# A hybrid decoder layer on one core: the split matrix products run high by high, high by low, low by high over all rows, instead of all three row by row

## The chip, the cores and the metric

One core of a Trainium2 chip runs the whole kernel. The metric is the device time of one execution in microseconds. In the text PE is TensorE, DVE is VectorE, ACT is ScalarE, POOL is GpSimd and SP is SyncE, which here only issues DMAs.

## The reference, cut to what matters

One layer of a decoder is computed for 1024 prompt tokens and 32 sample tokens, 1056 in all, with a model width of 1024. Everything is float32. The large products are these:

```
z = h @ w_in + b_in                                   # 1024 x 8192
q, f, i, og, glu_a, glu_b, gate_a, gate_b = split(z)
o_a = gated recurrence (HGRN2) of q, f, i, og         # small products per head
o_b = depthwise convolution of glu_a * sigmoid(glu_b), LayerNorm, silu
merged = [sigmoid(gate_a) * o_a, sigmoid(gate_b) * o_b] @ w_out     # 2048 x 1024
x = x + g1 * merged
gg, uu = split(h2 @ w_ffn_in)                         # 1024 x 5632
x = x + g2 * ((silu(gg) * uu) @ w_ffn_out)            # 2816 x 1024
y = rmsnorm(x, norm_final_w)
```

## The kernel before, in words

The wide products keep near float32 precision by splitting. A matrix A is rounded to `A_hi`, a shorter float (type fp32r), and `A_lo = A - A_hi`. A product is then the sum of `w_hi * x_hi`, `w_hi * x_lo` and `w_lo * x_hi`, three matmuls in place of one.

**Blocks.** The weights come in blocks of up to 8 row tiles of 128 rows by 128 columns (512 KB). For each block SP loads `w_raw`, ACT rounds it to `w_hi` (line 1776), and DVE, in a few places POOL, subtracts to get `w_lo` (lines 1281 and 2071). Each of these buffers exists twice, so while PE computes block b, block b+1 is prepared. ACT may write `w_hi` of block b only when block b-2 is done on PE, and SP may load into `w_raw` only when `w_lo` of block b-2 has been formed. The semaphore `w_hi_ready` counts the `w_hi` written, `w_split` the `w_lo`.

**The helper.** Every wide product after the first two tiles goes through `products` (line 865). It waits for `w_split`, and then runs over the row tiles `kt` of the block; for each row tile it issues high by high, high by low and low by high, each for all of its outputs. All matmuls have 128 rows, 128 columns of weights and 352 moving columns (`GW`, a third of the tokens), and each loads its own weights. Between row tiles it can call `at_slot`, which puts a small piece of other PE work (a "fill" of the recurrence, of the LayerNorm or of a norm) between the matmuls. `before_row` puts a wait ahead of a row tile.

**The stages.** (1) z: 64 tiles of the `w_in` product, each with three outputs in three PSUM banks (token groups g = 0, 1, 2), 72 matmuls per tile, for 8 heads of 7 tiles each and 8 tiles of `gate_b`; 62 of these go through `products`. Fills of the recurrence of the head before stand after row tiles 1, 3, 5 and 7. Before a tile is begun, PE waits for `z_free` of the tile two back, which the last reader of that PSUM tile gives. (2) Out: the `w_out` product, 3 token groups by 8 output tiles, each of two blocks (`kk`), with one output bank, 48 matmuls per tile. Its moving operand is `m_hi`/`m_lo`; at the first tile of a group PE waits row tile by row tile for `m_split`, which counts the `m_lo` that DVE formed (line 1539) from the `m_hi` of ACT (line 1942). (3) FFN: per token group 22 hidden tiles of two blocks each, then 8 output tiles of three blocks, one output bank per block. The first output tile of a group waits row tile by row tile for `a_ready`, the `act_lo` of the hidden tiles.

The program of each engine is a fixed order written out by hand, with loops (`Fori`) over heads and FFN tiles; semaphores alone tie the engines together.

## Time and profile before

| what | value |
|---|---|
| median of 3 runs | 2021.12 us (2020.4 to 2024.62) |
| profiled execution's own time | 2020.5 us |
| its span | 2018.8 us |
| PE busy | 1954.4 us, 97% of the span |
| PE weight loads busy | 1893.1 us, 94% |
| DVE busy | 1304.5 us, 65% |
| ACT busy | 671.3 us, 33% |
| POOL busy | 235.1 us, 12% |
| wide matmuls through line 876 | 10368 |

A row of the profile names the line, the engine, the operation and the tiles (output<-inputs). `PE` rows are matmuls and `PEld` rows the weight loads that run beside them. Matmuls overlap: a row's duration is longer than the distance to the next row's start, and the rate of PE is read from the starts. A bracket at a row's end gives the time that the engine had been idle and what released it.

### The profile page before, as it was taken

The page shows a single profiled execution, that of the slowest core. Times are in us where ns is not written, and L with a number is a line of the kernel's source. Part 1 is how long each engine was busy: PE and PEld are TensorE (multiplying, and loading weights), DVE is VectorE, ACT ScalarE, POOL GpSimd, SP SyncE. Part 2 cuts the span into 40 slices and gives each one's busy share as a digit, 9 for nine tenths or more (in the row PEclk, how much of TensorE's full clock was granted, in tenths as well). Part 3 has the DMA queues.
Part 4 walks back from the last instruction along what each step waited for, and adds up shares of the span by engine and source line. Part 5 has one row for each costly group of instructions (what it writes and reads, how often), then busy time and mean ns, then how long its engine had stood idle before and what let it go on. Part 6 is the DMA issues. An engine that isn't in the chain of part 4 may idle for free.

```text
span 2018.8 us, 39824 instructions
## 1 busy us (share of the span) xinstructions
PE 1954.4 (97%) x16182; PEld 1893.1 (94%) x16182; DVE 1304.5 (65%) x1800; ACT 671.3 (33%) x1090; POOL 235.1 (12%) x256
## 2 busy tenths in 40 slices
PE   7889999999999999999989989999999999999998
PEld 6888999999999999998989989999999999999998
DVE  6577969796978788887565655544446544455443
ACT  5211314132222313133664423333343333333333
POOL 2200010101010101011122484600000000000000
PEclk8999999999999999999999989999999999999999
DMA  8522232322222223223267634444444544444443
GB/s 244 193 71 68 65 89 65 85 69 69 75 78 75 79 64 88 65 65 97 89 211 215 193 100 136 137 141 136 135 138 136 155 132 137 136 142 150 142 127 113
DMA packets 417242, 237.40 MB, mean 118 GB/s; under 512 B 16375, under 2 KB 411287, under 8 KB 417072
## 3 DMA queue, kind: packets, MB, share of 16 engines
q1 hardware_dynamic: 416672, 234.48, 39.7%
q8 instruction: 115, 1.88, 0.4%
q10 hardware_dynamic: 416, 0.72, 0.1%
q14 instruction: 39, 0.32, 0.0%
HBM read 211.91 MB, written 24.11 MB: 117 GB/s over the span
## 4 chain that ended last, share of the span: by engine, by line
PE 82%; DVE 8%; ACT 3%; DMA 3%; POOL 2%; issue 1%; SPq 0%; DVEq 0%; ACTq 0%; POOLq 0%
PE Z L876 71%; DVE yb L1429 2%; PE R L900 2%; PE R L956 1%; DVE w_lo L1281 1%; PE Z L841 1%; PE R L906 1%; ACT w_hi L1776 1%; DVE ta L1446 1%; PE R L982 1%; PE R L989 1%; DMA mbuf<-merged_scratch 1%; DVE k L1310 1%; DMA w_raw<-in_w_in_dram 1%; PE R L991 1%
## 5 line engine op out<-in xcount | busy, mean ns | idle before, releaser
L876 PE MATMUL Z<-h_hi,w_hi 128*128 128x352 f32 x2544 | 684.3, 332 | 17.4 <-DVE w_lo L1281 9.7
L876 PE MATMUL Z<-h_hi,w_lo 128*128 128x352 f32 x2544 | 660.9, 323 | 0.0
L876 PE MATMUL Z<-h_lo,w_hi 128*128 128x352 f32 x2544 | 660.0, 323 | 0.0
L1776 ACT ACTIVATE w_hi<-w_raw 128x1024 fp32r<-128x1024 f32 (+1 forms) x316 | 329.3, 1042 | 962.7 <-PE Z L876 912.7
L1281 DVE TENSOR_TENSOR w_lo<-w_raw,w_hi 128x1024 fp32r<-128x1024 f32 (+1 forms) x305 | 378.6, 1241 | 393.3 <-ACT w_hi L1776 385.6
L876 PEld LDWEIGHTS Z<-h_hi,w_hi 128*128 128x128 f32 x2544 | 442.5, 189 | 36.9 <-issue 19.3
L876 PEld LDWEIGHTS Z<-h_hi,w_lo 128*128 128x128 f32 x2544 | 454.3, 189 | 0.0
L876 PEld LDWEIGHTS Z<-h_lo,w_hi 128*128 128x128 f32 x2544 | 452.4, 189 | 0.0
L1429 DVE SCALAR_TENSOR_TENSOR yb<-up,vec,yb 128x1024 f32 (+1 forms) x240 | 308.3, 1284 | 28.7 <-DVE yb L1429 3.7
L876 PE MATMUL Z<-act_hi,w_hi 128*128 128x352 f32 x528 | 170.9, 324 | 0.0
L876 PE MATMUL Z<-act_hi,w_lo 128*128 128x352 f32 x528 | 169.6, 321 | 0.0
L876 PE MATMUL Z<-act_lo,w_hi 128*128 128x352 f32 x528 | 169.3, 321 | 0.0
L876 PEld LDWEIGHTS Z<-act_hi,w_lo 128*128 128x128 f32 x528 | 99.4, 188 | 0.0
L876 PEld LDWEIGHTS Z<-act_lo,w_hi 128*128 128x128 f32 x528 | 99.2, 188 | 0.0
L876 PEld LDWEIGHTS Z<-act_hi,w_hi 128*128 128x128 f32 x528 | 99.0, 188 | 0.2 <-DVE w_lo L1281 0.2
L2154 POOL TENSOR_TENSOR gate<-ta,tb 128x1056 f32<-128x1056 f32 x8 | 20.9, 2615 | 668.1 <-ACT ta L1845 668.1
L1689 DVE TENSOR_TENSOR tb<-ta,Z 128x352 f32<-128x352 f32 x66 | 34.4, 521 | 74.3 <-PE Z L876 74.1
L876 PE MATMUL Z<-m_hi_b,w_hi 128*128 128x352 f32 x192 | 64.3, 335 | 4.5 <-POOL w_lo L2071 4.2
L876 PE MATMUL Z<-m_hi_a,w_hi 128*128 128x352 f32 x192 | 63.2, 329 | 3.5 <-DVE m_lo_a L1539 2.2
L876 PE MATMUL Z<-m_hi_b,w_lo 128*128 128x352 f32 x192 | 63.4, 330 | 0.0
L876 PE MATMUL Z<-m_lo_b,w_hi 128*128 128x352 f32 x192 | 63.2, 329 | 0.0
L876 PE MATMUL Z<-m_hi_a,w_lo 128*128 128x352 f32 x192 | 62.6, 326 | 0.0
(298 smaller groups left out, 2106.5 us busy)
## 6 DMA issues: line engine op xcount, KB each, us to landing
w_raw<-in_w_ffn_in_dram SPq DMA_DIRECT2D x132, 512.0 KB, 3.8
w_raw<-in_w_in_dram SPq DMA_DIRECT2D x64, 512.0 KB, 5.0
w_raw<-in_w_out_dram SPq DMA_DIRECT2D x48, 512.0 KB, 3.9
w_raw<-in_w_ffn_out_dram SPq DMA_DIRECT2D x48, 512.0 KB, 3.7
aw<-in_w_ada_dram SPq DMA_DIRECT2D x32, 512.0 KB, 4.0
w_raw<-in_w_ffn_out_dram SPq DMA_DIRECT2D x24, 384.0 KB, 3.3
ada_w<-in_w_ada_dram SPq DMA_DIRECT2D x16, 512.0 KB, 5.4
mbuf<-merged_scratch SPq DMA_DIRECT2D x32, 176.0 KB, 4.0
```

The lines of the kernel that those rows point to most:

```text
L841: last = mm(Z[b][:, g, 0:GW], w[:, kt, :], x[:, kt, g * GW:(g + 1) * GW], start=kt == 0 and m == 0, stop=kt == NJ - 1 and m == 2)
L876: last = mm(out, w[:, kt, :], x(kt, g), start=first and kt == 0 and m == 0, stop=last_block and kt == n - 1 and m == 2)
L900: return transpose(out, in_, ident[0:m, 0:m])
L906: last = mm(bank[group:group + 32, ADA_COL:ADA_COL + P], ct[:, kt, :], aw[:, kt, :], start=kt < 4, stop=kt >= 4)
L956: last = mm(bank[p:p + BAND, c * w:(c + 1) * w], k[:, t:t + BAND], halves(qd[:, t:t + BAND], 1 << lv, 1), start=True, stop=True)
L982: last = mm(bank[:, c * P:(c + 1) * P], ktok[:, cc, :], vtok[:, cc, :], start=True, stop=True)
L989: last = mm(out, att[:, cc, :], vtok[:, cc, :], start=True, stop=cc == 0)
L1281: st.tell(V.tensor_tensor(w_lo[b.par][:, 0:n, :], w_raw[b.par][:, 0:n, :], w_hi[b.par][:, 0:n, :].bitcast(F32), ALU.subtract), w_split, b. ...
L1429: ins = V.scalar_tensor_tensor(yp, xp, w, yp, ALU.mult, ALU.add)
L1689: st.tell(V.tensor_tensor(a, sg, Z[t.par][:, 1, 0:GW], ALU.mult), *zfree(t))
L1776: A(w_hi[b.par][:, 0:n, :], w_raw[b.par][:, 0:n, :], ACT.Copy).then_inc(w_hi_ready, 1)
L2154: st.tell(Q.tensor_tensor(gate[:, :], ta[:, :], tb[:, :], ALU.mult), gate_ready, h.v)
```

## The change

The row loop of `products` moves inside. The three kinds of product are now the outer loop, then the outputs, then the row tiles: all `w_hi * x_hi` of the block, then all `w_hi * x_lo`, then all `w_lo * x_hi`. The wait for `w_split` moves ahead of the third kind; ahead of the first stands a wait for `w_hi_ready`. Fills stay at the same count of matmuls within a block. In the z stage, where a block has three outputs, each output now gets its eight row tiles one after the other. The row waits are split likewise: `hi_row` waits for `m_hi_ready` or `a_hi_ready`, `lo_row` for `m_split` or `a_ready`. The first two z tiles, which have their own loop, are as before.

```diff
-            def products(b, outs, n, hi, lo, first, last_block, at_slot=None, slots=(), before_row=None):
+            def products(b, outs, n, hi, lo, first, last_block, at_slot=None, slots=(), hi_row=None, lo_row=None):
                 whi, wlo = w_hi[b.par], w_lo[b.par]
-                pe.wait_ge(w_split, b.v + 1)
-                for kt in range(n):
-                    if before_row is not None:
-                        before_row(kt)
-                    for m, (w, x) in enumerate(((whi, hi), (whi, lo), (wlo, hi))):
-                        for g, out in enumerate(outs):
+                count = 0
+                for m, (w, x, before_row) in enumerate(((whi, hi, hi_row), (whi, lo, lo_row), (wlo, hi, None))):
+                    if m == 0:
+                        pe.wait_ge(w_hi_ready, b.v + 1)
+                    if m == 2:
+                        pe.wait_ge(w_split, b.v + 1)
+                    for g, out in enumerate(outs):
+                        for kt in range(n):
+                            if before_row is not None:
+                                before_row(kt)
                             last = mm(out, w[:, kt, :], x(kt, g), start=first and kt == 0 and m == 0,
                                       stop=last_block and kt == n - 1 and m == 2)
-                    if kt == n - 1:
-                        last.then_inc(block_done, 1)
-                    for s in range(slots.count(kt)):
-                        at_slot()
+                            count += 1
+                            if count == 3 * len(outs) * n:
+                                last.then_inc(block_done, 1)
+                            if count % (3 * len(outs)) == 0:
+                                for s in range(slots.count(count // (3 * len(outs)) - 1)):
+                                    at_slot()
...
                              kk == 0, kk == 1, (lambda: x2_fill(g - 1, j)) if beside else None, (5,) if beside else (),
+                             (lambda kt: pe.wait_ge(m_hi_ready, M2 * g + NJ * kk + kt + 1)) if j == 0 else None,
                              (lambda kt: pe.wait_ge(m_split, M2 * g + NJ * kk + kt + 1)) if j == 0 else None)
...
-                def hidden(kk):
-
-                    return lambda kt: pe.wait_ge(a_ready, NF * g + 8 * kk + kt + 1)
+                def hidden(ready, kk):
+
+                    return lambda kt: pe.wait_ge(ready, NF * g + 8 * kk + kt + 1)
...
-                                 before_row=hidden(kk) if n == 0 else None)
+                                 hi_row=hidden(a_hi_ready, kk) if n == 0 else None,
+                                 lo_row=hidden(a_ready, kk) if n == 0 else None)
```

PE's program at a tile of the z stage, before (`h_hi` and `h_lo` are the moving operand, the numbers behind `w_hi` and `w_lo` tell the two buffers apart):

```order
244 L876 MATMUL Z<-h_hi,w_hi_68 128x352 [waits w_split,z_free1]
245 L876 MATMUL Z<-h_hi,w_hi_68 128x352 x2
246 L876 MATMUL Z<-h_lo,w_hi_68 128x352 x3
247 L876 MATMUL Z<-h_hi,w_lo_70 128x352 x3
248 L876 MATMUL Z<-h_hi,w_hi_68 128x352 x3
249 L876 MATMUL Z<-h_lo,w_hi_68 128x352 x3
250 L876 MATMUL Z<-h_hi,w_lo_70 128x352 x3
```

The same program in the changed kernel, at such a tile:

```order
177 L880 MATMUL Z<-h_hi,w_hi_68 128x352 [waits w_hi_ready,z_free1]
178 L880 MATMUL Z<-h_hi,w_hi_68 128x352 x23
179 L880 MATMUL Z<-h_lo,w_hi_68 128x352 x24
180 L880 MATMUL Z<-h_hi,w_lo_70 128x352 [waits w_split]
181 L880 MATMUL Z<-h_hi,w_lo_70 128x352 x23
```

The wait for `w_split` has moved from ahead of the first of 72 matmuls to ahead of the 49th; the wait for `z_free` stays at the first, and each x3 over three banks has become x8 in each bank.

PE's program at the begin of the out stage, before (`m_hi_a` and `m_hi_b` are the moving operands of a tile's two blocks):

```order
1406 L876 MATMUL Z<-m_hi_a,w_hi_67 128x352 [waits m_split,w_split,z_free0]
1407 L876 MATMUL Z<-m_lo_a,w_hi_67 128x352
1408 L876 MATMUL Z<-m_hi_a,w_lo_69 128x352
1409 L876 MATMUL Z<-m_hi_a,w_hi_67 128x352 [waits m_split]
1410 L876 MATMUL Z<-m_lo_a,w_hi_67 128x352
1430 L876 MATMUL Z<-m_hi_b,w_hi_68 128x352 [waits m_split,w_split]
1431 L876 MATMUL Z<-m_lo_b,w_hi_68 128x352
1432 L876 MATMUL Z<-m_hi_b,w_lo_70 128x352
```

The same place in the changed kernel:

```order
804 L880 MATMUL Z<-m_hi_a,w_hi_67 128x352 [waits m_hi_ready,w_hi_ready,z_free0]
805 L880 MATMUL Z<-m_hi_a,w_hi_67 128x352 [waits m_hi_ready] x7
806 L880 MATMUL Z<-m_lo_a,w_hi_67 128x352 [waits m_split] x8
807 L880 MATMUL Z<-m_hi_a,w_lo_69 128x352 [waits w_split]
808 L880 MATMUL Z<-m_hi_a,w_lo_69 128x352 x7
809 L880 MATMUL Z<-m_hi_b,w_hi_68 128x352 [waits m_hi_ready,w_hi_ready]
810 L880 MATMUL Z<-m_hi_b,w_hi_68 128x352 [waits m_hi_ready] x7
811 L880 MATMUL Z<-m_lo_b,w_hi_68 128x352 [waits m_split] x8
812 L880 MATMUL Z<-m_hi_b,w_lo_70 128x352 [waits w_split]
```

All eight row tiles of `m_hi` are now needed before the first of `m_lo`, and the low by high products come last.

## Rows read from the trace of the kernel before

**Rows 1.** The page, chain that ended last, by line.
```profile
PE Z L876 71%; DVE yb L1429 2%; PE R L900 2%; PE R L956 1%; DVE w_lo L1281 1%; PE Z L841 1%; PE R L906 1%; ACT w_hi L1776 1%; DVE ta L1446 1%; PE R L982 1%; PE R L989 1%; DMA mbuf<-merged_scratch 1%; DVE k L1310 1%; DMA w_raw<-in_w_in_dram 1%; PE R L991 1%
```
**Rows 2.** Waits of PE: who waited for whom, us in total, times, longest.
```profile
PE Z L876 <- DVE w_lo L1281: 11.1, 6, 5.9
...
PE Z L876 <- POOL w_lo L2071: 4.2, 1, 4.2
...
PE Z L876 <- DVE m_lo_a L1539: 2.2, 1, 2.2
```
**Rows 3.** Timeline, first wide tile: start us, us, engine, line, operation, tiles [idle<-releaser].
```profile
78.94 1.06 ACT L1776 ACTIVATE w_hi<-w_raw 128x1024 fp32r<-128x1024 f32 x1 [7.13 <-DMA w_raw<-in_w_in_dram]
79.90 1.12 ACT L1829 ACTIVATE tb<-Z,vec 128x1056 f32<-128x1056 f32 x1
80.03 1.23 DVE L1281 TENSOR_TENSOR w_lo<-w_raw,w_hi 128x1024 fp32r<-128x1024 f32 x1 [8.40 <-ACT w_hi L1776]
...
81.37 0.50 PEld L876 LDWEIGHTS Z<-h_hi,w_hi 128*128 128x128 f32 x2 [6.17 <-ACT tb L1829]
```
**Rows 4.** Timeline, third and fifth wide tile.
```profile
110.32 1.22 DVE L1281 TENSOR_TENSOR w_lo<-w_raw,w_hi 128x1024 fp32r<-128x1024 f32 x1 [9.68 <-ACT w_hi L1776]
...
128.26 0.95 PE L876 MATMUL Z<-h_hi,w_hi 128*128 128x352 f32 x2 [4.68 <-DVE q L1467]
```
**Rows 5.** Timeline, begin of the out stage, each engine.
```profile
1023.93 3.19 ACT L1942 ACTIVATE m_hi_a<-x 128x352 fp32r<-128x352 f32 x8
1024.51 5.12 DVE L1539 TENSOR_TENSOR m_lo_a<-x,m_hi_a 128x352 fp32r<-128x352 f32 x8 [0.18 <-ACT m_hi_a L1942]
1029.56 7.92 DVE L1539 TENSOR_TENSOR m_lo_b<-x,m_hi_b 128x352 fp32r<-128x352 f32 x8
1030.87 1.04 ACT L1776 ACTIVATE w_hi<-w_raw 128x1024 fp32r<-128x1024 f32 x1
1034.67 0.66 PE L876 MATMUL Z<-m_hi_b,w_hi 128*128 128x352 f32 x1 [4.24 <-POOL w_lo L2071]
1035.83 0.50 ACT L1942 ACTIVATE m_hi_b<-x 128x352 fp32r<-128x352 f32 x1 [2.50 <-POOL x L2188]
```
**Rows 6.** Windows: us, busy us (x) of PE, PEld, DVE, ACT, POOL, granted clock, DMA.
```profile
1034.60:1040.50 5.90, 5.83 (x24) 5.83 (x25) 4.01 (x6) 1.44 (x2) 1.19 (x2) 0.62 0.67 203
```
**Rows 7.** Timeline, two later tiles of the out stage.
```profile
1067.73 0.43 PE L876 MATMUL Z<-m_hi_b,w_hi 128*128 128x352 f32 x1 [0.26 <-DVE w_lo L1281]
...
1086.20 1.06 ACT L1776 ACTIVATE w_hi<-w_raw 128x1024 fp32r<-128x1024 f32 x1 [2.72 <-DMA w_raw<-in_w_out_dram]
...
1088.66 0.40 PE L876 MATMUL Z<-m_hi_a,w_hi 128*128 128x352 f32 x1 [1.17 <-DVE w_lo L1281]
```
**Rows 8.** Timeline, FFN stage, the two tiles that waited.
```profile
1520.77 0.40 PE L876 MATMUL Z<-h_hi,w_hi 128*128 128x352 f32 x1 [0.39 <-DVE w_lo L1281]
...
1779.85 0.40 PE L876 MATMUL Z<-h_hi,w_hi 128*128 128x352 f32 x1 [0.63 <-DVE w_lo L1281]
```
**Rows 9.** Timeline of PE, z stage between two fills, first and last of five.
```profile
515.24 0.64 PE L876 MATMUL Z<-h_lo,w_hi 128*128 128x352 f32 x3
...
517.18 0.65 PE L876 MATMUL Z<-h_hi,w_lo 128*128 128x352 f32 x3
```
**Rows 10.** Timeline of PE, out stage, first and last of 19.
```profile
1113.97 0.32 PE L876 MATMUL Z<-m_hi_a,w_hi 128*128 128x352 f32 x1
...
1116.87 0.32 PE L876 MATMUL Z<-m_hi_a,w_hi 128*128 128x352 f32 x1
```
**Rows 11.** Timeline of PE, FFN group 0, first and last of 27.
```profile
1299.80 0.32 PE L876 MATMUL Z<-h_hi,w_hi 128*128 128x352 f32 x1
...
1303.93 0.32 PE L876 MATMUL Z<-h_hi,w_lo 128*128 128x352 f32 x1
```
**Rows 12.** Timeline of PE, FFN group 1, first and last of 27.
```profile
1649.70 0.32 PE L876 MATMUL Z<-h_hi,w_hi 128*128 128x352 f32 x1
...
1653.86 0.32 PE L876 MATMUL Z<-h_hi,w_lo 128*128 128x352 f32 x1
```

More of the change, by code:

```diff
@@ L862, in _, with z_tile @@
             first_tiles()
-            def products(b, outs, n, hi, lo, first, last_block, at_slot=None, slots=(), before_row=None):
+            def products(b, outs, n, hi, lo, first, last_block, at_slot=None, slots=(), hi_row=None, lo_row=None):
                 whi, wlo = w_hi[b.par], w_lo[b.par]
-                pe.wait_ge(w_split, b.v + 1)
-                for kt in range(n):
-                    if before_row is not None:
-                        before_row(kt)
-                    for m, (w, x) in enumerate(((whi, hi), (whi, lo), (wlo, hi))):
-                        for g, out in enumerate(outs):
+                count = 0
[8 more added lines that the diff above has]
+                                before_row(kt)
                             last = mm(out, w[:, kt, :], x(kt, g), start=first and kt == 0 and m == 0,
                                       stop=last_block and kt == n - 1 and m == 2)
-                    if kt == n - 1:
-                        last.then_inc(block_done, 1)
-                    for s in range(slots.count(kt)):
-                        at_slot()
-            def z_tile(b, at_slot=None, slots=(), before_row=None):
+                            count += 1
[4 more added lines that the diff above has]
+                                    at_slot()
+            def z_tile(b, at_slot, slots):
                 t = b
@@ L887, in z_tile @@
                          lambda kt, g: h_hi[:, kt, g * GW:(g + 1) * GW], lambda kt, g: h_lo[:, kt, g * GW:(g + 1) * GW],
-                         True, True, at_slot, slots, before_row)
+                         True, True, at_slot, slots)
             def small(fill):
```

## The prediction

> **What bounds the kernel now.** I read the page first, then PE's waits, then the timeline around each wait, then PE's starts in undisturbed stretches. The chain that ended last is 71% wide matmuls of line 876 [rows 1], and PE is busy for 97% of the span: the kernel is a stream of 10368 equal matmuls with few holes. Two things can move it: the holes that the new waits close, and the distance between starts within the stream. One nanosecond more or less per matmul is 10.4 us, more than all the holes of this kind together.
>
> The holes that the change aims at are small. PE waited 11.1 us in 6 places for DVE's `w_lo`, 4.2 us in one for POOL's, and 2.2 us in one for `m_lo_a` [rows 2]: 17.5 us. What counts is what would be late next in each.
>
> **The holes, one by one.**
>
> *First wide tile.* `w_hi` was there at 78.94 + 1.06 = 80.00, `w_lo` at 80.03 + 1.23 = 81.26, and the weight load began at 81.37, 0.11 later. But the tile writes into the bank that ACT was reading into `tb` until 79.90 + 1.12 = 81.02 [rows 3], and the wait for `z_free` stays. The new start is about 81.12. Of 5.9 us only 0.25 is gained, the rest was the DMA.
>
> *Third to fifth tile.* The third tile waited for its `w_lo` too, but the fifth waited 4.68 us for DVE's `q`; DVE works without a pause from 110.32 to it, and what started DVE was a `w_hi` that came with its DMA [rows 4]. Starting the third tile earlier only lengthens that wait: 0.
>
> *The other z tiles.* The list has no further wait for `w_lo` there. Fills keep their place by count, and DVE's order is as before: 0.
>
> *Begin of the out stage.* Before, the first block followed `m_lo_a` row tile by row tile and ended three matmuls after the last, near 1030.3, and the second waited for POOL's `w_lo` until 1034.67 [rows 5]. Now the first block's high pass starts at about 1024.45, behind the first `m_hi`, and is paced by ACT to 1023.93 + 3.19 = 1027.1; the low pass is paced by DVE to 1024.51 + 5.12 = 1029.6; then come eight more matmuls, 1.3 us: end at 1031.1, 0.8 later than before. The second block needs `w_hi` (1030.87 + 1.04 = 1031.9), runs seven row tiles, and waits for the eighth `m_hi_b`, made at 1035.83 + 0.50 = 1036.33, where before that row was asked for last. Its low pass waits for the last `m_lo_b` at 1029.56 + 7.92 = 1037.5 at the least, and the third pass takes 1.3: end at 1039.0, against 1040.5 before [rows 6], a gain of 1.4. Before, this block ran at a granted clock of 0.62 [rows 6], its slow matmuls 0.293 us apart where the fast ones are 0.160. If after the new hole of 2.9 us it runs at the half clock again, 16 matmuls at 0.293 are 4.7 us, and the end is 1041.2: a loss of 0.8. I take half of the first: 0.7.
>
> *Later in the out stage.* A row lasts two steps, 0.32 us, so a hole in the starts is the idle time plus one step of 0.16. At 1067.73 it is 0.26 + 0.16 = 0.4, and `w_lo` caused it [rows 7]: gained, since `w_lo` is now due 16 matmuls, 2.5 us, after the start. At 1088.66 `w_hi` itself was late with its DMA, done at 1086.20 + 1.06 = 1087.26 [rows 7]; PE can start at 1087.37: 1.3 gained, `w_lo` and the next load come no later.
>
> *FFN.* The hole ahead of 1520.77 is 0.39 + 0.16 = 0.55, that ahead of 1779.85 0.63 + 0.16 = 0.8 [rows 8]. `w_hi` was long there; both go. The row waits for `act_hi` and `act_lo` caused none before, and the last hidden tile is asked for 5 matmuls into the third block, 7.7 + 0.8 us on: none now.
>
> Sum: 0.25 + 0.7 + 0.4 + 1.3 + 0.55 + 0.8 = 4.0 us. Ends: 2.5 (out stage at its worst) and 4.7. If each closed hole opened again as another wait, 0.
>
> More register work and waits on PE stand in the loops. The sequencer runs ahead of the stream, and waits that are met ride on a weight load; no row shows a cost: 0.
>
> **The step.** Starts between which nothing intervenes lie at different distances. z: 12 matmuls from 515.24 to 517.18 are 161.7 ns each [rows 9]; of the fourteen such stretches from 500 to 560 us nine read so, five near 160.0, mean 161.1. Out: 18 steps in 2.90 us, 161.1 [rows 10]. FFN group 0: 26 steps in 4.13 us, 158.8 [rows 11]. Group 1: 26 in 4.16, 160.0 [rows 12]. The granted clock is full in all. DVE, ACT and POOL being busy or not makes no difference that I could find. After an interruption the stream locks at one of three rates and keeps it until the next. The changed order has another pattern (the same kind eight times, and in z one bank at a time instead of three in turn), so the trace of before does not show its rate. Present weights: z 4464 at 161.1, FFN groups 0 and 2 3168 at 158.8, group 1 1584 and out 1152 at about 160.0, together 1660.0 us, mean 160.1. Bounds: all at 158.8 is 13.6 us less, all at 161.1 is 10.3 more, all at z's 161.7 is 16.4 more. I take 160.0, the middle rate and nearest to the mean: z loses 4.9, groups 0 and 2 gain 3.8, in all 1.1 less.
>
> The Trainium skill, page TensorE: Matmul & The Clock Gate, section "Wait — 56ns, not 53.3ns?", has a start-to-start distance of columns over 2.4 GHz plus a fixed 2.5 ns, which no order of the matmuls would alter; for 352 columns that is an estimate of 149.2 ns, and these rows are 10 to 12 ns above and differ among themselves. By that rule the step term is nil and the sum is the holes alone.
>
> **Sum.** The profiled execution took 2020.5 us, 0.6 under the median. 2020.5 - 4.0 - 1.1 = 2015.4 us, 0.28% under the median. A difference of 0.2%, 4.0 us, is about what a measurement of this kernel can tell from none: faster is under 2017.1, slower over 2025.2.
>
> **Rivals.**
> - *The step does not depend on the order*, each stage keeps its rate: 2020.5 - 4.0 = 2016.5. For it: the same operations with the same loads. Against it: rates that differ between stages now. (The page's rule above gives this one.)
> - *All streams lock at the fast rate* of FFN group 0: 2020.5 - 4.0 - 13.6 = 2002.9. For it: one bank per pass is now true everywhere, and the longest undisturbed stretches with one bank are at 158.8. Against it: group 1 and the out stage, with one bank, are not.
> - *All lock slow*, at 161.1 or above, slower than before. The place is the FFN stage, where 3168 matmuls now run at 158.8 and lose 7.3; with group 1 and out it is 10.3, 2020.5 - 4.0 + 10.3 = 2026.8, and up to 2033 at 161.7. It decides from a common step of 160.9 (8.7 us more). For it: the out stage shows 161.1 with one bank; every weight load is now a new one, where before two matmuls in a row shared `w_hi`. Against it: loads are issued for each matmul anyway.
> - *The change doesn't do what it says*: the holes move (to `z_free`, to `m_hi_b`, to the next DMA) and nothing is gained: about 2020. The first tiles are such a case already; the four later holes have no second wait that I can find.
>
> **Chances.** Forecast (2011 to 2019) 0.40; step unchanged 0.20; fast lock, and half-way to it, 0.15; slow lock 0.14; holes only move 0.11. From these: faster 0.32 + 0.11 + 0.15 = 0.58; slower the slow lock's, 0.14; same the rest, 0.28. The range leaves out the ends of both locks: 2004 to 2026. The forecast's own range is 2011 to 2019.
>
> **What would show it.** PE's waits for `w_lo` after the first tile gone, the weight load of the first wide tile begun for ACT's `tb`, the wait for `q` at 128 still there and longer; a hole ahead of the last `m_hi_b` row near 1033; no hole where 1067, 1088, 1520 and 1779 were. Starts in the z stage 160 ns apart, in FFN group 0 up from 158.8. I am wrong if the FFN groups lie at 161 or at 158 throughout, or if PE's total of waits does not fall by some 4 us.

## The result: slower by 0.24%

| | median | runs | lowest to highest |
|---|---|---|---|
| kernel before | 2021.32 us | 12 | 2017.41 to 2024.62 |
| changed kernel | 2025.48 us | 12 | 2023.35 to 2029.19 |

The ratio is 1.0024, with a 95% interval of 1.0016 to 1.0031. The forecast was 2015.4 us, with a range of 2004 to 2026. The time lies just inside the range, on the side that had 0.14: the rival "all lock slow" came true, a little under its price of 2026.8. The change was forecast as a gain and is a small loss.

The profiled execution of the changed kernel took 2029.19 us (span 2027.5), the slowest of its twelve, 3.7 over the median; that of before lay 0.8 under its own. So the traces differ by 8.7 us of span where the medians differ by 4.2. The rest of this section is read from the two traces. Each experiment was timed beside further runs of the kernel before on the same chip, and its ratio refers to these; their medians were 2021.47 us for `e1` to `e4`, 2021.08 for `e5` to `e8`, 2021.55 for `e9` to `e12`, and 2022.83 for `e13` and `e14`.

The page of the changed kernel, busy time of the engines, and the chain that ended last by line (answers to [rows 1]):

```profile
PE 1967.7 (97%) x16182; PEld 1906.0 (94%) x16182; DVE 1306.0 (64%) x1800; ACT 671.3 (33%) x1090; POOL 234.0 (12%) x256
...
PE Z L880 73%; DVE yb L1437 2%; PE R L906 2%; DVE w_lo L1289 1%; PE R L962 1%; PE Z L841 1%; ACT w_hi L1784 1%; PE R L912 1%; DVE ta L1454 1%; PE R L988 1%; PE R L995 1%; DMA w_raw<-in_w_out_dram 1%; DMA w_raw<-in_w_in_dram 1%; DVE k L1318 1%; PE R L997 1%
```

The same 16182 matmuls keep PE busy for 13.3 us more (1954.4 before). The waits of PE, all rows of the view added up, fell from 56.6 to 52.0 us. 13.3 less 4.6 is 8.7, the whole difference of the spans. The holes closed as the forecast had it; the stream between them became slower.

**The waits.** The same view as [rows 2], of the changed kernel (who waited for whom, us in total, times, longest):

```profile
PE Z L880 <- ACT tb L1837: 5.5, 1, 5.5
PE Z L880 <- ACT w_hi L1784: 3.5, 2, 2.1
PE Z L880 <- ACT v L1841: 2.7, 1, 2.7
PE Z L880 <- DVE tb L1475: 2.6, 1, 2.6
PE Z L880 <- DVE q L1475: 2.2, 1, 2.2
PE Z L880 <- ACT m_hi_b L1950: 2.1, 1, 2.1
```

No row of line 880 names `w_lo` any more (one of 0.8 us is left in the loop of the first two tiles, as before); before, `w_lo` and `m_lo_a` made 17.5 us. In their place stand `tb` at the first tile, `v` and `tb` at the next ones, `w_hi` and `m_hi_b` in the out stage. The first wide tile, answering to [rows 3] (timeline, columns as there):

```profile
80.38 1.06 ACT L1784 ACTIVATE w_hi<-w_raw 128x1024 fp32r<-128x1024 f32 x1 [7.00 <-DMA w_raw<-in_w_in_dram]
...
81.34 1.12 ACT L1837 ACTIVATE tb<-Z,vec 128x1056 f32<-128x1056 f32 x1
81.46 1.22 DVE L1289 TENSOR_TENSOR w_lo<-w_raw,w_hi 128x1024 fp32r<-128x1024 f32 x1 [8.27 <-ACT w_hi L1784]
...
82.51 0.79 PEld L880 LDWEIGHTS Z<-h_hi,w_hi 128*128 128x128 f32 x3 [5.75 <-ACT tb L1837]
```

`tb` ends at 82.46 and PE starts 0.05 later, while `w_lo` is ready only at 82.68. The load starts 0.17 ahead of `w_lo`, where before it started 0.11 behind it: 0.28 gained, 0.25 forecast.

The begin of the out stage, answering to [rows 5], and behind it the window that answers to [rows 6] (busy us of PE, PEld, DVE, ACT, POOL, then granted clock and DMA):

```profile
1027.94 3.06 PE L880 MATMUL Z<-m_hi_a,w_hi 128*128 128x352 f32 x8 [0.79 <-ACT m_hi_a L1950]
...
1034.85 0.50 ACT L1950 ACTIVATE m_hi_b<-x 128x352 fp32r<-128x352 f32 x1 [2.81 <-POOL x L2196]
...
1036.14 1.04 ACT L1784 ACTIVATE w_hi<-w_raw 128x1024 fp32r<-128x1024 f32 x1
...
1037.24 2.09 PE L880 MATMUL Z<-m_hi_b,w_hi 128*128 128x352 f32 x7 [2.14 <-ACT w_hi L1784]
...
1041.38 0.66 PE L880 MATMUL Z<-m_hi_b,w_hi 128*128 128x352 f32 x1 [2.05 <-ACT m_hi_b L1950]
```

```profile
1037.00:1046.00 9.00, 6.71 (x27) 6.25 (x28) 3.40 (x4) 3.17 (x6) 3.54 (x2) 0.62 0.50 148
```

The hole ahead of the eighth `m_hi_b` is there as forecast, and with it the half clock. In this execution the next tile begins at 1045.61, 17.7 us after the stage's first matmul, where before it was 14.6 (1025.98 to 1040.61): 3.0 lost, against 0.7 forecast as a gain. Part of that is `w_hi`: ACT took it only behind the `m_hi_b` that waited for POOL's `x`. Another part is the clock, which was at half twice here, before (1032.3 to 1039.1) once:

```profile
1030.80:1034.20 3.40, 3.40 (x13) 3.40 (x13) 3.21 (x8) 1.24 (x4) 2.92 (x1) 0.50 0.92 275
1037.60:1044.50 6.90, 4.85 (x18) 4.39 (x17) 3.14 (x3) 2.44 (x4) 3.20 (x2) 0.51 0.49 154
```

The loss is not one of every execution. `e3`, `e7` and `e13` below have the same order and waits at this place, and their first tile takes 14.6, 14.6 and 15.2 us; that of `e14`, which has the same waits, takes 17.6. After its first tile the out stage is 4.1 us shorter than before (189.4 for 193.5). PE's wait of 4.4 us for POOL's `rs`, which the prediction did not name, is gone there, one for DVE's `ysum` is 1.9 longer, and the clock was at half once (6.8 us) where before it was twice (10.3 us).

Later in the out stage, answering to [rows 7]:

```profile
1092.46 1.06 ACT L1784 ACTIVATE w_hi<-w_raw 128x1024 fp32r<-128x1024 f32 x1 [3.06 <-DMA w_raw<-in_w_out_dram]
...
1093.66 0.56 PE L880 MATMUL Z<-m_hi_a,w_hi 128*128 128x352 f32 x2 [1.34 <-ACT w_hi L1784]
```

The hole of 1088 is still there, now for `w_hi` alone and its DMA: the block came later in the DMA queue, and the gain of 1.3 is not to be seen. The holes of 1067, 1520 and 1779 [rows 7, 8] are gone.

**The step.** Four windows of the changed kernel inside the FFN stage, in which PE is never idle and the granted clock is 1.00; the first two lie in group 0 (`h` rows, then hidden rows), the last two in group 1:

```profile
1260.00:1380.00 120.00, 120.00 (x744) 120.00 (x743) 62.04 (x78) 44.11 (x62) 32.24 (x42) 1.00 0.47 135
1410.00:1480.00 70.00, 70.00 (x435) 70.00 (x434) 28.07 (x31) 22.63 (x26) 0.00 (x0) 1.00 0.48 137
1600.00:1650.00 50.00, 50.00 (x317) 50.00 (x317) 25.37 (x34) 18.56 (x26) 0.00 (x0) 1.00 0.47 138
1680.00:1740.00 60.00, 60.00 (x373) 60.00 (x372) 25.14 (x29) 19.61 (x23) 0.00 (x0) 1.00 0.47 138
```

The number in brackets behind PE counts the matmuls that touch the window. A matmul's row is two steps long, so some two of them lie over the edges, and the step is the window by the count less two: 120 / 742 is 161.7 ns, 70 / 433 is 161.7, 60 / 371 is 161.7, but 50 / 315 is 158.7. One matmul more or less is 0.2 ns in the first window and 0.5 in the third. The same from the starts in the timeline of group 0: these two rows are 13 passes of eight matmuls apart, 104 steps in 16.82 us, 161.7:

```profile
1300.97 1.46 PE L880 MATMUL Z<-h_hi,w_lo 128*128 128x352 f32 x8
...
1317.79 1.46 PE L880 MATMUL Z<-h_hi,w_hi 128*128 128x352 f32 x8
```

Before, this stretch ran at 158.8 [rows 11]. In the z stage the rows before [rows 9] stand against these of a tile without fills, 24 steps in 3.88 us, 161.7:

```profile
665.42 4.04 PE L880 MATMUL Z<-h_lo,w_hi 128*128 128x352 f32 x24
669.30 4.04 PE L880 MATMUL Z<-h_hi,w_lo 128*128 128x352 f32 x24
```

The steps of each stage, worked out from all starts of the wide matmuls in a trace (distances of over 180 ns, and the first three of a stretch, left out), are the measure for the experiments. How the stretches are bounded moves such a mean by up to 0.2 ns. Those of before and after, in ns:

| | z | out | FFN 0 | FFN 1 | FFN 2 |
|---|---|---|---|---|---|
| matmuls | 4464 | 1152 | 1584 | 1584 | 1584 |
| before | 161.12 | 160.18 | 158.90 | 159.92 | 159.03 |
| after | 161.34 | 161.40 | 161.66 | 160.60 | 161.63 |
| difference, us | 1.0 | 1.4 | 4.4 | 1.1 | 4.1 |

Together 12.0 us, most of the 13.3 by which PE is busier. The lengths of the stages, from first matmul to first matmul (the last one to its last matmul), say the same of the FFN stage: its groups took 253.2, 258.9 and 262.2 us before and 257.4, 259.3 and 265.4 after, 7.8 more. `e7` and `e13`, with the order of the changed kernel, repeat its three lengths within 0.3 us. What else differs between these executions lies ahead of the FFN stage.

A mean of 159.92 or 160.60 in group 1 is a mixture: a stream keeps a constant rate over stretches of tens of microseconds, and one and the same order shows several such rates. In the stages with one output they are 158.9, 160.0 and 161.1 before, 161.7 and 158.3 after. And the rate can change in mid-stream. In the changed kernel the 32 steps from the first of these rows to the second are 158.4 ns each, the 16 from the second to the third 161.9, with nothing between them:

```profile
1661.24 1.43 PE L880 MATMUL Z<-h_hi,w_lo 128*128 128x352 f32 x8
...
1666.31 1.46 PE L880 MATMUL Z<-act_hi,w_hi 128*128 128x352 f32 x8
...
1668.90 1.46 PE L880 MATMUL Z<-act_hi,w_lo 128*128 128x352 f32 x8
```

### The profile page after: what moved, and what is told of

Read it like the earlier page. It is cut to its first block, busy times and chain, and to the rows that moved or that the text cites. A ratio compares the mean times of both kernels' runs of the same rounds, so it can differ in the third digit from the quotient of the medians.

```text
span 2027.5 us, 39824 instructions
## 1 busy us (share of the span) xinstructions
PE 1967.7 (97%) x16182; PEld 1906.0 (94%) x16182; DVE 1306.0 (64%) x1800; ACT 671.3 (33%) x1090; POOL 234.0 (12%) x256
## 4 chain that ended last, share of the span: by engine, by line
PE 84%; DVE 8%; ACT 3%; DMA 2%; issue 1%; POOL 1%; DVEq 0%; SPq 0%; ACTq 0%; POOLq 0%
PE Z L880 73%; DVE yb L1437 2%; PE R L906 2%; DVE w_lo L1289 1%; PE R L962 1%; PE Z L841 1%; ACT w_hi L1784 1%; PE R L912 1%; DVE ta L1454 1%; PE R L988 1%; PE R L995 1%; DMA w_raw<-in_w_out_dram 1%; DMA w_raw<-in_w_in_dram 1%; DVE k L1318 1%; PE R L997 1%
## 5 line engine op out<-in xcount | busy, mean ns | idle before, releaser
L880 PE MATMUL Z<-h_hi,w_hi 128*128 128x352 f32 x2544 | 470.5, 332 | 14.5 <-ACT tb L1837 5.5
L880 PE MATMUL Z<-h_lo,w_hi 128*128 128x352 f32 x2544 | 454.2, 325 | 0.0
L880 PE MATMUL Z<-h_hi,w_lo 128*128 128x352 f32 x2544 | 452.4, 325 | 0.0
L880 PEld LDWEIGHTS Z<-h_hi,w_lo 128*128 128x128 f32 x2544 | 414.1, 188 | 4.7 <-issue 3.9
L880 PEld LDWEIGHTS Z<-h_lo,w_hi 128*128 128x128 f32 x2544 | 414.2, 189 | 0.7 <-issue 0.2
L880 PE MATMUL Z<-act_hi,w_hi 128*128 128x352 f32 x528 | 98.7, 325 | 0.0
L880 PE MATMUL Z<-act_hi,w_lo 128*128 128x352 f32 x528 | 97.0, 324 | 0.0
L880 PE MATMUL Z<-act_lo,w_hi 128*128 128x352 f32 x528 | 97.0, 324 | 0.0
L1317 DVE TENSOR_TENSOR qd<-qd,tot 128x512 f32<-128x512 f32 (+1 forms) x48 | 33.1, 690 | 39.0 <-PE R L962 39.0
L880 PE MATMUL Z<-m_hi_b,w_hi 128*128 128x352 f32 x192 | 36.2, 330 | 4.2 <-ACT w_hi L1784 2.1
```

The costliest lines, as they stand in the source:

```text
L880: last = mm(out, w[:, kt, :], x(kt, g), start=first and kt == 0 and m == 0, stop=last_block and kt == n - 1 and m == 2)
L1317: st.do(V.tensor_tensor(late, late, pairs[:, :, 0:1].to_broadcast(shape), ALU.mult))
```

## The experiments

The theory is that the order alone sets the step. The rival was that the waits, or a disturbance of this one execution, made the loss. All kernels compute the whole result except `e7` and `e8`. They differ in `products` only (`e12` in where buffers lie instead), which is written with a function `one(m, kt, g)` that issues the matmul of kind `m` (0 is high by high, 1 high by low, 2 low by high), row tile `kt` and output `g`; `n` is the number of row tiles, `N` that of outputs. The short forms leave out the row waits and the fills. The fills keep their count of matmuls within the block; the row waits are those of the changed kernel where a stage has a new order, and the old ones where it has not.

### The order without the new waits: e1

Here the row waits are the old ones too.

```diff
-pe.wait_ge(w_hi_ready, b.v + 1)
+pe.wait_ge(w_split, b.v + 1)
 for m in range(3):
-    if m == 2:
-        pe.wait_ge(w_split, b.v + 1)
     for g in range(N):
         for kt in range(n):
             one(m, kt, g)
```

> The new order of the matmuls with the old waits: w_split ahead of the first matmul of a block, m_split and a_ready ahead of the high by high rows. Theory A (the step of the single-bank streams costs about 8 us and the new waits give back about 4): 2028 to 2030 us, 1.003 to 1.0045 of before, FFN starts 161.7 ns apart. Rival B (the new waits are what costs, by opening other holes such as the one for ysum at the third token group; the step is chance): 2020 to 2022 us, no slower than before.

Measured: 2029.69 us, 1.0040 [1.0026, 1.0053] of before. So the order alone costs 8.1 us, as theory A expected. By the difference of the ratios (1.0040 less 1.0024) the new waits give back 3.2 us; worked out from the two intervals, that is uncertain by 3.1. The steps are those of the changed kernel: 161.31, 161.41, 161.66, 160.60, 161.60. Its waits for `w_lo` are back:

```profile
PE Z L873 <- DVE w_lo L1311: 12.3, 6, 5.9
```

### One stage at a time: e2 and e3

```diff
+if N == 3: by kind, new waits      # e2; in e3 this is the order before
+else: by row tile, old wait        # e2; in e3 this is the new order
```

> The new order and waits in the z stage alone, the old ones in the out and FFN stages. Theory A (the FFN and out stages lose): within 2 us of before, 2020 to 2023 us, starts in the z stage 161.3 ns apart on the mean as in the changed kernel, FFN group 0 back at 158.9. Rival C (one bank at a time in the z stage is what costs): the 4 us of the changed kernel, 2025 us.

> The old order in the z stage, the new one in the out and FFN stages. Theory A: as the changed kernel, 2024 to 2026 us, FFN starts 161.7 ns apart. Rival C (the z stage costs): as before, 2021 us or, with the holes closed, 2018 us.

Measured: `e2` 2021.22 us, 0.9996 [0.9986, 1.0006]; `e3` 2024.68, 1.0013 [1.0003, 1.0023]. Steps of `e2`: 161.33 in z, and 159.73, 159.02, 159.98, 159.03 after it. Of `e3`: 161.10 in z, and 160.83, 161.66, 161.56, 161.64 after it. Both times are as theory A expected. By and large each stage takes its step from its own order, and the loss is in the stages with one output. One thing crosses the stages: the fast stretch at 1600 us, present in the changed kernel and in `e1`, is missing in the profiled execution of `e3`, which has the same order there and another z stage:

```profile
1600.00:1650.00 50.00, 50.00 (x311) 50.00 (x310) 25.17 (x33) 18.19 (x26) 0.00 (x0) 1.00 0.47 138
```

### The closed holes with other orders: e4 and e5

```diff
+for kt in range(n): one(0, kt); one(1, kt)                       # e4
+pe.wait_ge(w_split, b.v + 1)
+for kt in range(n): one(2, kt)
```

```diff
+for kt in range(n + 4):                                          # e5, out and FFN only
+    if kt < n: one(0, kt); one(1, kt)
+    if kt == 4: pe.wait_ge(w_split, b.v + 1)
+    if kt >= 4: one(2, kt - 4)
```

> Each block in two passes: row tile by row tile high by high and high by low, then all low by high; w_split is waited for ahead of the second pass, as in the changed kernel's third. If the slow step comes from consecutive matmuls with the same kind of operand and a new row tile each time (theory A1), the pairs of the first pass lie nearer to 158.9 and the time is 2015 to 2020 us. If every order but that of before locks slowly (A2): 2022 to 2026 us with FFN starts at 161 or above.

> The z stage as before. In the out and FFN stages the row by row order is kept, but low by high of a row tile comes four row tiles later, so w_split is due 12 to 14 matmuls into the block and not at its first. Theory A1 (the step belongs to the alternation of the kinds, not to the waits): FFN starts 158.9 apart, the holes closed, 2016 to 2018 us, 0.998 of before. Rival A2 (any order but that of before locks slower): 160.5 to 161.7, 2022 us or more.

Measured: `e4` 2018.39 us, 0.9988 [0.9977, 0.9999]; `e5` 2017.72, 0.9986 [0.9977, 0.9996]. Steps of `e4`: 161.02, 160.43, 160.51, 160.27, 160.58; of `e5`: 161.16, 160.12, 159.82, 160.19, 159.86. Both times lie in the range of theory A1, but the steps do not fit it as well: the FFN of `e4` at 160.3 to 160.6 lies between its 158.9 and the 161 of A2, nearer to A2, and that of `e5` at 159.8 to 160.2 and not at 158.9. In `e5` `w_split` is due after 10 matmuls of a block, not after 12 to 14. The late wait for `w_split` is worth its few microseconds as soon as the order does not take them away; the intervals reach to 0.9999 and 0.9996, so this much is just shown.

### The z stage bank by bank: e6

```diff
+for g in range(3):                  # z only; out and FFN as before
+    for kt in range(n):
+        for m in range(3): one(m, kt, g)
```

> The out and FFN stages and all waits as before. In the z stage each bank gets its 24 products in one go, row tile by row tile with the three kinds inside, the very pattern of the FFN stage. Theory A1: z starts go from 161.1 to about 159.2 on the mean (fills re-lock it every 18 matmuls), 4464 x 1.9 = 8 us less: 2012 to 2014 us. Rival D (the z stage is slow because of its fills and not of its order): 161 again, 2021 us.

Measured: 2017.35 us, 0.9976 [0.9964, 0.9988], about half of the gain expected by theory A1 (2012 to 2014 us). The z step is 159.76, 1.4 under before; 1.9 was expected. With the three kinds of a row tile next to each other, leaving out the rotation over three banks gains; the changed kernel leaves it out as well and gains nothing (161.34), so it is not the rotation alone that sets the z step. What the rotation costs by itself no run shows. The FFN stage of `e6` is that of before to the letter, and yet its hidden rows in group 0 ran at 161.1 and not at 158.9 (x374 in 60 us for x379), and its `h` rows in group 1 at 161.1 and not at 160.0. So the rates of one order also vary from one kernel to the next.

### Which operand: e7 and e8

```diff
-last = mm(out, w[:, kt, :], x(kt, g), ...)
+last = mm(out, w[:, 0, :], x(kt, g), ...)      # e7, out and FFN
+last = mm(out, w[:, kt, :], x(0, g), ...)      # e8, out and FFN
```

Here the products of the out and FFN stages are computed with the first row tile of one operand in place of all eight.

> The changed kernel, but in the out and FFN stages every weight load takes row tile 0 of its block, so only row tile 0 of the weights enters the sums. If the slow step comes from the weights' address moving on with each load: FFN starts 161.7 go to 159 or below. If the moving operand's address matters: they stay at 161.7.

> The changed kernel, but in the out and FFN stages every matmul of a pass streams row tile 0 of its moving operand, so only that one enters the sums. If the moving operand's row stride makes the slow step: FFN starts go to 159 or below. If the weights' address does: 161.7 again. If neither this nor the run with the same weights changes the step, it is the sequence of kinds alone.

One run each: `e7` 2022.96 us, `e8` 2017.89. Windows of `e7`, then of `e8`:

```profile
1260.00:1380.00 120.00, 120.00 (x744) 120.00 (x744) 61.94 (x80) 44.30 (x62) 26.50 (x35) 1.00 0.47 135
```

```profile
1260.00:1380.00 120.00, 120.00 (x752) 120.00 (x751) 64.30 (x79) 44.46 (x63) 27.80 (x36) 1.00 0.47 137
1600.00:1650.00 50.00, 50.00 (x318) 50.00 (x317) 24.71 (x33) 18.61 (x27) 0.00 (x0) 1.00 0.48 138
1850.00:1900.00 50.00, 50.00 (x312) 50.00 (x311) 24.50 (x33) 18.55 (x26) 0.00 (x0) 1.00 0.47 137
```

With the same weights 744 matmuls fit, as in the changed kernel; with the same moving row tile 752, 160.0 ns each. The expectation for `e8` named 159 or below and 161.7, and this is neither. In `e8` the starts in that stretch are all 160 ns apart, where in the changed kernel the distances repeat every four matmuls: 158 or 159, 159 or 160, 164, 165. The steps of `e8` by stage are 161.28, 159.69, 159.88, 159.08, 160.64, and again they are mixtures: the second and third row give 158.2 and 161.3, from starts 158.3 and 161.1, with one row tile in every pass. The stretches at 158.3 repeat every four matmuls too (158, 161, 155, 159), so a repeat of four does not need four addresses. What is shown is that with the walk of the moving operand the 161.7 goes away, while the walk of the weights has no part in it (`e7` has the steps of the changed kernel throughout the FFN stage).

### The two faster orders together: e9 and e10

`e10` is `e5` with the z stage of `e6`. `e9` has that z stage too; in out and FFN the low by high product of the first three row tiles comes at the end of the block:

```diff
+for kt in range(n):
+    one(0, kt); one(1, kt)
+    if kt == 3: pe.wait_ge(w_split, b.v + 1)
+    if kt >= 3: one(2, kt)
+for kt in range(3): one(2, kt)
```

> z runs bank by bank, three kinds per row tile. In the out and FFN stages each row tile runs high by high and high by low at once and low by high from the fourth row tile on; the low by high products of the first three row tiles come last. Theory (the step follows the order in which the moving row tiles are visited, and is short where a row tile is visited several times in a row): z near 159.8 as in the run bank by bank, out and FFN between 158.9 and 160 except over the last three matmuls of each block, where the row changes each time; w_lo holes closed, no late row wait from the low pass. Total 2017.4 (bank by bank alone) less up to 3: 2014.5 to 2017. Rival (the step is locked at an interruption and the order within a block matters little): each stage as in the kernel before, 2017.4. Rival (any irregular order costs): FFN at 161, 2024.

> The two orders that were each faster, together: z bank by bank (2017.35, 4.0 under before), out and FFN row by row with low by high four rows later (2017.72, 3.6 under before). If the two gains are independent: 2021.2 - 4.0 - 3.6 = 2013.6, steps 159.8 in z, 159.8 to 160.2 after it. Rival (both gain from one thing, or the bank by bank order ends z so that out and FFN lock otherwise): 2017.5. Either way not slower than the faster of the two by more than 0.1%.

Measured: `e9` 2012.61 us, 0.9951 [0.9937, 0.9965]; `e10` 2013.65, 0.9956 [0.9944, 0.9969]. Both beat the kernel before by more than the interval, and the changed kernel by 0.7%. The two gains add; `e10` took the 2013.6 that were expected for that. The steps of `e9` are 159.66 in z and 160.19, 160.27, 159.94, 160.39 after it, those of `e10` 159.81 and 160.09, 159.81, 160.19, 159.86. For the FFN of `e9` the expectation was 158.9 to 160; it came out a little above, and the time a little below the expected 2014.5 to 2017.

### What about the walk: e11, e12, e13

The row tiles of `h` and `m` are 4224 bytes apart in a partition, those of the hidden tensors 1408. By 512 these leave 128 and 384: from row tile to row tile the start address moves by a quarter of 512 bytes and takes four residues (remainders by 512) in turn. That the starts repeat every four matmuls as well gave the idea, no more. Four row tiles further the residue is the same again. The `hi` and `lo` buffers of `h` and of `m` lie 33792 bytes or three times that apart, a multiple of 512, so in the order before the three kinds of a row tile had one residue (158.9 in group 0), while the three outputs of z, 1408 bytes apart, moved it by a quarter two times in three (161.1), and bank by bank they did not (`e6`, 159.8).

```diff
-for kt in range(n):
+for kt in (0, 4, 1, 5, 2, 6, 3, 7):   # e11; (0, 4, 1, 5, 2, 3) in a block of six
+for kt in (0, 5, 2, 7, 4, 1, 6, 3):   # e13; (0, 5, 2, 3, 4, 1) in a block of six
```

```diff
-act_hi, act_lo = at("act_hi", [P, NF, GW], F32R, B1), ...
+act_hi, act_lo = at("act_hi", [P, NF, 384], F32R, B1), ...    # e12: rows 1536 bytes apart
```

The buffers grow by this, so `e12` also moves the buffer for the output rows to another place.

> The changed kernel, except that in the out and FFN stages each pass visits its row tiles in the order 0 4 1 5 2 6 3 7 (0 4 1 5 2 3 in a block of six). Row tiles of the moving operand are 4224 bytes apart in h and m and 1408 in the hidden tensors, so four rows further is a multiple of 512 bytes, and the start address modulo 512 now changes at every second matmul instead of at each. Theory (the 161.67 with its repeat of four matmuls comes of the walk of the moving start address over its four residues): the repeat of four becomes one of eight or goes, and the FFN step falls, by half of the distance to the same row (160.0 or 158.4) or more: 160.9 or less, total 2025.4 - 0.8 x 5.9 = 2020.7 or less. Rival (it is only that the row changes at all, whatever its address): step stays at 161.67, total 2025.4.

> The changed kernel with the row tiles of the two hidden tensors 1536 bytes apart instead of 1408, a multiple of 512, so that the start address of the moving operand has the same residue in every row. Only the second half of each FFN group (the matmuls that read the hidden tensors, 1584 in all) is touched. Theory (residue walk makes 161.67): there the step falls to 160.0 or 158.4, the first half of each group stays at 161.67: 1584 x 1.67 ns = 2.6 us to 1584 x 3.3 = 5.2 us less than the changed kernel, 2022.8 to 2020.2. Rival (any change of row costs, or the pattern is not of addresses): 161.67 in both halves, 2025.4.

> A control for the permuted rows: the changed kernel, but each pass of the out and FFN stages visits its row tiles in the order 0 5 2 7 4 1 6 3 (0 5 2 3 4 1 in a block of six). That is as irregular in rows as 0 4 1 5 2 6 3 7 (2018.13 us, step 160.0), but the start address modulo 512 bytes again changes by one quarter at every matmul, as in the changed kernel. Theory (the walk of the residue makes the slow step): FFN steps back at 161.67 with the same repeat of four, total near 2025. Rival (the plain ascending order of neighbouring rows makes it, any other order breaks it): 160.0, total near 2018.

Measured: `e11` 2018.13 us, 0.9982 [0.9973, 0.9991]; `e13` 2024.53, 1.0009 [0.9999, 1.0020]; `e12` 2021.99, 1.0005 [0.9995, 1.0015]. Windows of `e11`, of `e13` and of `e12`:

```profile
1260.00:1380.00 120.00, 120.00 (x752) 120.00 (x752) 63.45 (x79) 45.22 (x64) 28.84 (x37) 1.00 0.47 138
1410.00:1480.00 70.00, 70.00 (x440) 70.00 (x439) 30.36 (x34) 23.06 (x28) 0.00 (x0) 1.00 0.47 135
1600.00:1650.00 50.00, 50.00 (x314) 50.00 (x313) 24.79 (x33) 18.74 (x27) 0.00 (x0) 1.00 0.47 137
```

```profile
1260.00:1380.00 120.00, 120.00 (x745) 120.00 (x744) 62.01 (x78) 44.32 (x62) 25.50 (x33) 1.00 0.46 135
1410.00:1480.00 70.00, 70.00 (x435) 70.00 (x434) 30.10 (x34) 23.20 (x27) 0.00 (x0) 1.00 0.47 137
1600.00:1650.00 50.00, 50.00 (x318) 50.00 (x317) 25.36 (x33) 18.56 (x26) 0.00 (x0) 1.00 0.47 138
```

```profile
1260.00:1380.00 120.00, 120.00 (x744) 120.00 (x744) 61.56 (x78) 44.27 (x62) 29.89 (x39) 1.00 0.46 135
1410.00:1480.00 70.00, 70.00 (x436) 70.00 (x436) 28.73 (x32) 22.63 (x26) 0.00 (x0) 1.00 0.46 133
1600.00:1650.00 50.00, 50.00 (x318) 50.00 (x317) 25.61 (x34) 19.17 (x28) 0.00 (x0) 1.00 0.49 143
```

`e11` and `e13` are both irregular orders of the same rows. The time of `e11` lies under the 2020.7 of its theory, that of `e13` near the expected 2025. Where the residue changes at every second matmul, the step is 160.0 in every stage with one output, the fast stretch of group 1 included (314 matmuls for 317). Where it changes at every matmul, the steps are as in the changed kernel: 161.67 in group 0 with the same repeat of four, and the fast stretch at 1600 too. Its FFN groups take 257.4, 259.3 and 265.1 us, those of `e11` 254.7, 258.4 and 263.0. The ratio of `e13`, 1.0009, is a little under the 1.0024 of the changed kernel; the intervals overlap. The order of the rows as such does nothing; the quarter step of the residue at each matmul does. The unit need not be 512 bytes. Rows four further leave the same by 512 and not by 1024, which excludes 1024; the rows leave the same by 128 always, which excludes 128. But 256 fits the two runs as well: by it the residue has two values, which alternate at each matmul in the changed kernel and in `e13` and change at every second in `e11`. No run separates 512 from 256.

`e12` is half a hit. In groups 0 and 1, where the hidden rows follow the `h` rows without a pause, they run at 161.1, under 161.7 but not at 160.0 or 158.4. In group 2 they do so too up to the first fill of the last tiles, and from that break on it is 160.0, where the changed kernel has 161.6. Its rows there (one of six matmuls is left out), 24 steps from the first start to the last in 3.84 us, 160.0:

```profile
1964.69 1.12 PE L880 MATMUL Z<-act_hi,w_lo 128*128 128x352 f32 x6
1965.65 1.12 PE L880 MATMUL Z<-act_hi,w_hi 128*128 128x352 f32 x6
1966.61 1.12 PE L880 MATMUL Z<-act_lo,w_hi 128*128 128x352 f32 x6
...
1968.53 1.44 PE L880 MATMUL Z<-act_hi,w_hi 128*128 128x352 f32 x8
```

One may take this for a stream that keeps the rate of the `h` rows ahead of it until it is interrupted. The traces speak against it: the hidden rows of `e12` run at 161.1 behind `h` rows at 161.7 (group 0) and behind `h` rows at 158.3 (group 1), and `e8`, where nothing changes ahead of them, goes from 161.1 to 160.0 at the same fill. `e8` and the hidden rows of `e12` both have one residue for all rows of a pass, and they share these two rates, and at 161.1 the same repeat of six (158, 159, 161, 162, 162, 165, each within 1 ns). So a constant residue does away with 161.7 and leaves it open which of the other rates a stretch takes. The total, 3.5 us under the changed kernel, lies in the expected 2020.2 to 2022.8.

### All stages with the permuted rows: e14

```diff
-for kt in range(n):
+for kt in (0, 4, 1, 5, 2, 6, 3, 7):   # as e11, in z too
```

> The changed kernel with the row order 0 4 1 5 2 6 3 7 in all stages, z too. Theory (residue walk): z, where each bank runs its eight rows in a pass, falls from 161.3 to about 160.0: 4464 matmuls x 1.3 ns = 5.8 us less than with the permuted rows in out and FFN alone, 2018.1 - 5.8 = 2012.3, so 0.45% under the kernel before. Rival (z's rate comes of its many interruptions or of the change of banks, not of the rows): z stays at 161.3, total 2018.1.

Measured: 2013.39 us, 0.9958 [0.9946, 0.9971]. The z step is 160.05, and the others 159.99, 160.00, 160.02, 160.05. Two rows of a z tile, 24 steps in 3.83 us, 159.6:

```profile
659.28 3.99 PE L873 MATMUL Z<-h_lo,w_hi 128*128 128x352 f32 x24
663.11 4.01 PE L873 MATMUL Z<-h_hi,w_lo 128*128 128x352 f32 x24
```

This is the changed kernel with nothing but its row tiles visited in another order, and it is 0.66% faster than it (1.0024 less 0.9958, 13 us). Worked out from the two intervals, the 0.66% is uncertain by 0.15, 3 us. By the steps it should be 4464 x 1.29 + 1152 x 1.41 + 1584 x (1.66 + 0.58 + 1.58) ns = 5.8 + 1.6 + 6.1 = 13.5 us. The expectation had 160.0 for z and 2012.3 us. These are the steps that the prediction assumed, 160.0 everywhere, and its sum was 0.28% under before; the kernel that has them is 0.42% under it, with an interval of 0.29 to 0.54.

## Why the prediction was wrong, step by step

- **The holes: right in sum, not in each place.** 4.0 us were forecast. The waits fell by 4.6 in the trace, 4.3 of them waits of the wide matmuls, and `e1` against the changed kernel gives 3.2. The first tile came out as worked (0.28 for 0.25), and the holes of 1067, 1520 and 1779 are gone. Wrong were two places: the hole of 1088 stayed, as the block's DMA came later too, and the begin of the out stage lost 3.0 in this execution, where the clock was at half twice. Wrong as well that the wait for `q` at the fifth tile would be longer: it is 2.2 for 4.7 [rows 4], with 2.6 for `tb` and 2.7 for `v` at the tiles around it. That the sum fits is in part luck.
- **The step: the term that failed.** The prediction put it as "I take 160.0, the middle rate and nearest to the mean", 1.1 us less. It measured 12.0 us more: z did not fall to 160.0 but rose to 161.34, and FFN groups 0 and 2 went to 161.6. With 12.0 in place of -1.1 the prediction's own sum is 2028.5 us, and the profiled execution took 2029.19. With the order alone, `e1` has 8.1 us more in the timed runs. The prediction had the lever right (10.4 us for a nanosecond) and the bounds as well; the value between them was a mean over rates of another order, and the order that was coming had a property that none of these had in full: the start residue of the moving operand moves by a quarter of 512 bytes at every matmul. Before, z had it for two of three and ran at 161.1, with 161.7 in nine of fourteen stretches [rows 9]; of the rows at hand these were the nearest to the order that was coming.
- **"After an interruption the stream locks at one of three rates and keeps it until the next"** does not hold in full. The changed kernel goes from 158.3 to 161.7 at 1666.31 without an interruption, where the `h` rows end and the hidden rows begin.
- **"All lock slow": right in place and in direction,** the FFN stage at 161 and more, put at 2026.8. It measured 2025.48. Two stretches (1109 to 1117 and 1586 to 1666 us) even ran at 158.4, and yet the step cost 12.0 and not the 10.3 of this rival, since the others locked at 161.7 and not at 161.1. Its argument for it, that every weight load is now a new one, is refuted by `e7`. The argument against the forecast that was at hand was the pitch of the buffers, which stands in the code; the chance of 0.14 took no note of it.
- **"The step does not depend on the order"** fell: the same operations with the same weight loads measured 12.0 us more of step.
- **The page of the Trainium skill.** By the rule of the Trainium skill, page TensorE: Matmul & The Clock Gate, section "Wait — 56ns, not 53.3ns?", which has no term for the order, an estimate for 352 columns is 149.2 ns. The traces do not agree: the rates of the streams lie between 158.3 and 161.7, and the measurement decides.
- **"The holes only move"** is refuted by the sum of waits; `e1` against the changed kernel says the same, at the edge of its uncertainty.

Left open is what chooses among the rates that one order can have: 161.7 and 158.3 for the order of the changed kernel, 158.9, 160.0 and 161.1 for that before, 158.3, 160.0 and 161.1 with one row tile. The profiled executions of the changed kernel, `e1`, `e7`, `e8`, `e12` and `e13` all have a stretch of 158.3 at the same place in group 1, and that of `e3` has not, which speaks against chance. Open too is the unit of the residue. The hidden rows before are a hint: there `act_hi` and `act_lo` lie half of 512 bytes apart, so by 512 the residue changes at each matmul, by 256 only from row to row, as in the `h` rows; and in groups 0 and 2 they hold the same 158.9 as the `h` rows. That is what 256 bytes would give, but no run was made for it. What the mechanism in the chip is no run shows.

## What to carry to other kernels

When a stream of matmuls bounds a kernel, read the distance between starts in each stage before, and do not take a mean over rates of one order for the rate of another. Work out how the start address of the moving operand walks in the new order. In this kernel an order that moves it by a quarter of 512 bytes at every matmul ran mostly at 161.7 ns, one per cent over the 160.0 of the same order with its rows visited in pairs of one residue. Where a kernel's streams do the same, visiting the rows in such pairs is a change of one line. A wait that moves off the front of a block is worth its idle time only, here 3 to 5 us, and half a nanosecond of step undoes it.

## What the runs showed of the hardware that was not expected

- 128 x 128 by 352 matmuls with a weight load each ran at a few distinct rates, at a granted clock of 1.00, and the order of the moving rows sets which rates occur. Start residue moved by a quarter of 512 bytes at each matmul: 161.7 ns, or in some stretches 158.3 (changed kernel, `e1`, `e7`, `e13`). Rows in pairs of one residue: 160.0 in every stage (`e14`), as in `e11` for the stages with one output. The same row, or one residue for all rows: 161.1, 160.0 and 158.3 in different stretches (`e8`; 161.1 and 160.0 in `e12`). The order before, in the stages with one output: 158.9, 160.0 and 161.1.
- The addresses of the weights made no difference here (`e7`: 161.66 in FFN group 0, and the lengths of the three groups as in the changed kernel).
- The rate changed in mid-stream, without a break, where one moving tensor followed another: from 158.3 to 161.7 in the changed kernel, from 161.7 or 158.3 to 161.1 in `e12`.
- The two profiled executions of the changed kernel and of `e13`, with steps that are equal within 0.2 ns in every stage, have spans of 2027.5 and 2019.7 us; their FFN groups agree within 0.3 us. A single trace tells a step of 0.1 ns over a long stretch but not a total to better than some microseconds.
